# A hybrid recurrence and feed-forward block: second norm turned by DMA inside SBUF, first transfers issued ahead of the parity branch

## The chip, the cores and the metric

The kernel runs on the 8 cores of one Trainium2 chip. Its time is the device time, in microseconds, of the slowest core; the figure for a kernel is the median of its runs. Cores 0 to 3 are one die, cores 4 to 7 the other. Even and odd cores run two different programs of one kernel, chosen by a branch on the parity of the core's number.

## What is computed

The input x is 4 sequences of 4096 tokens, 1024 wide, in float32. Cut to what matters:

```python
h = rmsnorm(x, norm_mix_g)
q, f, i, g, c, bg, xb, ga, gb = split(h @ w_in)       # 4x512, 3x512, 2x1024
y_a = hgrn2_mixer(q, f, i, g) @ w_branch_a           # gated linear recurrence, 4 heads of 128x128
y_b = (bg * causal_conv3(c * xb)) @ w_branch_b       # depthwise, 3 taps
x = x + (sigmoid(ga) * y_a + sigmoid(gb) * y_b) @ w_out
h2 = rmsnorm(x, norm_ffn_g)                          # "the second norm"
x = x + (silu(h2 @ w_gate) * (h2 @ w_up)) @ w_down   # inner width 2816
out = rmsnorm(x, norm_final_g)
```

## The kernel before, in words

Each pair of cores takes one sequence. The even core computes its first 2152 tokens, the odd core the last 1944. The recurrence carries a state over the whole sequence, so the odd core first runs a short pre-scan over the tokens before its own (projections f and i only), which gives it the state to begin with; the even core has no such part. `BL_EVEN` and `BL_ODD` (lines 18 and 19) cut the tokens into blocks of tiles, as (tiles, rows of a tile): even (4,128), (4,128), (3,128), (3,128), (3,120); odd (4,128) three times and (4,102). The pre-scan of the odd core uses the even cut.

All matmuls are bf16 with float32 sums in PSUM, which has 8 banks of 512 columns. Most projections have the weights as the stationary operand and 128 channels of up to 512 tokens as the moving one (`mm_fm`, line 823, its matmuls recorded at L830); some are token-major (`mm_tok`, L841). Weights lie in HBM as float32 slabs of 128x4096 (2 MB), and are cast to bf16 on the way into a ring of 8 slots by DMAs that the pool engine issues (`load_next`, line 697, recorded at L714 and in tables as ring<-wall). Their order is `LOADS` (line 418). A slab is loaded into a slot once its former user has released it; the first slabs are cut in quarters, and a quarter can be gated on the arrival of an x tile.

The stages: (1) the first norm. An x tile (128 tokens by 1024 channels, 512 KB) is loaded by SP (`load_more`, line 742, L747, ring<-xall); ACT squares and sums it, ACT makes the reciprocal root, DVE scales it into bf16, and `transp` (line 852) turns it: TensorE transposes eight 128x128 pieces into a PSUM bank (L859) and DVE multiplies them by the norm weight on the way to `hT` (L810). (2) conv projections (`conv_gen`, line 1047), beside the norm of the next block; on odd cores also the pre-scan (`pf_gen`, `pt_gen`, `pv_gen`). (3) per block the dense projections of the recurrence and its core, merged with the first half of the gates (`gates_gen`, line 1313). (4) the second half of the gates of block b+1, merged with `d_gen` of block b (line 1358): the output projection, the residual sum x1, its store to HBM (`x1spill`, L1378), the load of the next x tile (L1354), and the second norm. For each pair of tiles this is a square and a reciprocal root on ACT, a scaling on DVE into one of two buffers in `rtmp`, and `transp` into `hT`. The buffer of a tile is also what the square of the tile after next writes. (5) the feed-forward projections (`ffn_gen`, line 1410); the last block of stage 4 is merged with their start. (6) the down projection with the final norm (`down_gen`, line 1437).

The order on each engine is fixed at build time. The generators are merged by their costs (`merge`, line 371) into a list of operations with their reads and writes; `schedule` (line 180) then plays the list through a model: each operation has a duration, a DMA takes its `nbytes` at `DMA_RATE` = 310e3 bytes a microsecond and `DMA_LAT` = 2.2 us more, and the next operation of an engine is the one that can start first. `pick` gives each PSUM result the bank that was freed longest ago (two neighbouring banks where a result needs a pair). `run` (line 309) issues the order, with a wait on a semaphore for each dependency not yet known to be met. Each of the five engine queues takes the branch in `emit_both` (line 339) first, and everything of the program stands behind it.

At the start six small ACT operations (L774 to L778) and two on DVE make the constants of the forget gate. They stand ahead of the first norm in the list.

## Time and profile before

| | us |
|---|---|
| median of 3 runs (lowest, highest) | 1015.64 (1014.77, 1016.02) |
| the profiled execution | 1016.44 |
| its span, core 4 (first to last instruction of the slowest core) | 1014.9 |
| spans of even cores 0, 2, 6 | 1011.2, 1010.7, 1011.0 |
| spans of odd cores 1, 3, 5, 7 | 1011.2, 1012.0, 1009.9, 1009.5 |
| busy on core 4: TensorE, DVE, ACT | 974.9, 435.5, 376.3 |

Times below are in us from the span's start on the core named. PE is TensorE; SPq, POOLq and the like are an engine's own queue; "issue" is time in which the profile shows nothing that the engine waits for. "[3.16 <-DMA ring<-wall]" behind a row is the time that the engine sat idle before it, and what ended that.

### The profile page before, as it was taken

The page shows a single profiled execution, that of the slowest core. Times are in us where ns is not written, and L with a number is a line of the kernel's source. Part 1 is how long each engine was busy: PE and PEld are TensorE (multiplying, and loading weights), DVE is VectorE, ACT ScalarE, POOL GpSimd, SP SyncE. Part 2 cuts the span into 40 slices and gives each one's busy share as a digit, 9 for nine tenths or more (in the row PEclk, how much of TensorE's full clock was granted, in tenths as well). Part 3 has the DMA queues.
Part 4 walks back from the last instruction along what each step waited for, and adds up shares of the span by engine and source line. Part 5 has one row for each costly group of instructions (what it writes and reads, how often), then busy time and mean ns, then how long its engine had stood idle before and what let it go on. Part 6 is the DMA issues. An engine that isn't in the chain of part 4 may idle for free.

```text
span 1014.9 us, 15424 instructions; the slowest of 8 cores (1009.5 to 1014.9 us)
## 1 busy us (share of the span) xinstructions
PE 974.9 (96%) x5574; PEld 526.6 (52%) x5574; DVE 435.5 (43%) x678; ACT 376.3 (37%) x668; POOL 24.6 (2%) x52
## 2 busy tenths in 40 slices
PE   0889999999999999999999999999999999999997
PEld 0435646455556554455555645555464655444455
DVE  3535467776877664566544212122221212223223
ACT  3434285948586742445534111111111111111112
POOL 2000000000000000000000000000000000000000
PEclk9999999999999999999999999999999999999999
DMA  6982405100003544334387040203003053323112
GB/s 125 237 199 46 79 1 94 33 1 2 1 1 55 113 97 112 116 119 140 124 176 150 1 84 1 43 1 64 21 5 79 2 125 125 125 106 119 63 63 59
DMA packets 18947, 78.74 MB, mean 78 GB/s; under 512 B 2224, under 2 KB 2224, under 8 KB 15792
## 3 DMA queue, kind: packets, MB, share of 16 engines
q0 software_dynamic: 6336, 33.03, 18.5%
q1 hardware_dynamic: 12393, 44.38, 13.2%
q8 instruction: 49, 0.80, 0.3%
q14 instruction: 34, 0.28, 0.1%
q10 hardware_dynamic: 135, 0.25, 0.1%
HBM read 93.05 MB, written 17.63 MB: 109 GB/s over the span
## 4 chain that ended last, share of the span: by engine, by line
PE 90%; DMA 4%; ACT 2%; issue 2%; DVE 1%; SPq 1%; POOL 0%; ACTq 0%; DVEq 0%; POOLq 0%
PE pf L830 60%; PE pf L1454 16%; PE pf L841 10%; DMA ring<-wall 3%; DMA ring<-xall 1%; ACT arena L806 1%; PE pf L859 1%; PE pf L1079 1%; SPq L747 0%; ACT L806 0%; PE pf L1254 0%; PE pf L1256 0%; PE pf L1215 0%; PE pf L1234 0%; PE pf L1304 0%
## 5 line engine op out<-in xcount | busy, mean ns | idle before, releaser
L830 PE MATMUL pf<-hT,ring 128*128 128x384 bf16 (+2 forms) x3200 | 607.8, 346 | 6.4 <-DMA ring<-wall 3.2
L830 PEld LDWEIGHTS pf<-hT,ring 128*128 128x128 bf16 x3200 | 311.9, 98 | 273.2 <-issue 11.3
L1454 PE MATMUL pf<-ring,arena 128*128 128x512 bf16 (+2 forms) x735 | 159.8, 373 | 0.0
L806 ACT ACTIVATE rtmp<-pf 128x512 f32<-128x512 f32 (+2 forms) x114 | 59.9, 531 | 203.2 <-PE pf L830 196.5
L1454 PEld LDWEIGHTS pf<-ring,arena 128*128 128x128 bf16 (+1 forms) x735 | 76.2, 105 | 78.1
L810 DVE TENSOR_TENSOR arena<-rtmp,pf 128x512 bf16<-128x512 f32 (+2 forms) x85 | 51.7, 609 | 143.1 <-PE pf L830 129.5
L806 ACT ACTIVATE arena<-pf 128x512 f32<-128x512 f32 (+11 forms) x145 | 77.7, 572 | 75.5 <-PE pf L830 68.8
L830 PE MATMUL pf<-arena,ring 128*128 128x512 bf16 (+2 forms) x320 | 70.8, 345 | 1.5 <-ACT arena L806 1.4
L806 ACT ACTIVATE rtmp<-hT 128x1024 bf16<-128x1024 f32 (+3 forms) x19 | 18.4, 967 | 130.7 <-DVE hT L810 130.7
L841 PE MATMUL pf<-ring,hT 128*128 128x512 bf16 (+1 forms) x272 | 62.6, 379 | 0.0
L806 ACT ACT_TABLE_LOAD x44 | 56.5, 1283 | 6.6 <-DVE sso L1262 3.7
L841 PE MATMUL pf<-ring,arena 128*128 128x512 bf16 (+1 forms) x248 | 58.4, 379 | 0.0
L810 DVE TENSOR_TENSOR hT<-pf,hT 128x512 f32<-128x512 f32 (+2 forms) x35 | 23.7, 676 | 80.3 <-PE pf L1454 80.3
L818 DVE SCALAR_TENSOR_TENSOR arena<-arena,pf 128x512 f32<-128x512 f32 (+2 forms) x54 | 32.2, 600 | 34.9 <-PE pf L830 23.4
L806 ACT ACTIVATE rtmp<-arena 128x1024 bf16<-128x1024 f32 (+4 forms) x27 | 27.0, 1000 | 51.9 <-DVE arena L818 51.9
L810 DVE TENSOR_TENSOR hT<-pf,cst_sb 128x1024 bf16<-128x1024 bf16 (+1 forms) x34 | 40.4, 1206 | 9.0 <-PE pf L859 8.9
L830 PEld LDWEIGHTS pf<-arena,ring 128*128 128x128 bf16 x320 | 30.4, 98 | 26.0 <-issue 1.8
L810 DVE TENSOR_TENSOR arena<-U,pf 128x512 bf16<-128x512 f32 (+2 forms) x27 | 16.3, 604 | 62.0 <-PE pf L830 60.1
L841 PEld LDWEIGHTS pf<-ring,hT 128*128 128x128 bf16 (+1 forms) x272 | 28.1, 104 | 28.1
L714 POOL DMA_DIRECT2D ring<-wall x44 | 23.4, 532 | 791.3 <-PE pf L830 590.8
L810 DVE TENSOR_TENSOR arena<-arena 128x512 bf16<-128x512 f32 (+8 forms) x46 | 36.9, 801 | 9.2 <-ACT arena L806 6.6
L810 DVE TENSOR_TENSOR arena<-Wt,pf 128x512 bf16<-128x512 f32 (+2 forms) x25 | 15.1, 603 | 56.9 <-PE pf L830 56.9
(101 smaller groups left out, 572.9 us busy)
## 6 DMA issues: line engine op xcount, KB each, us to landing
ring<-wall POOLq DMA_DIRECT2D x24, 1024.0 KB, 11.4
ring<-xall SPq DMA_DIRECT2D x14, 512.0 KB, 8.7
arena<-xall SPq DMA_DIRECT2D x14, 512.0 KB, 4.4
x1spill<-arena SPq DMA_DIRECT2D x14, 512.0 KB, 3.0
hT<-x1spill SPq DMA_DIRECT2D x14, 512.0 KB, 4.4
out<-hT SPq DMA_DIRECT2D x14, 512.0 KB, 2.6
ring<-wall POOLq DMA_DIRECT2D x12, 256.0 KB, 10.6
ring<-wall POOLq DMA_DIRECT2D x6, 512.0 KB, 5.8
```

The source lines that it names most:

```text
L714: P.dma("pool", lambda E, s=s, idx=idx, a=a, z=z: E.dma_start(out=ring[s][:, a:z], in_=w_d[idx][:, a:z]), reads=need(gates[q]) if q < len( ...
L806: P.op("act", lambda E: E.activation(out=rs(out), in_=rs(in_), func=func, **kw), reads=reads, writes=writes, dur=dur, aset=ASET[func] if f ...
L810: P.op("dve", lambda E: E.tensor_tensor(out=rs(out), in0=rs(a), in1=rs(b), op=op), reads=reads, writes=writes, dur=0.17 + width(out, a, b) ...
L818: P.op("dve", lambda E: E.scalar_tensor_tensor(out=rs(out), in0=rs(a), scalar=s, in1=rs(b), op0=op0, op1=op1), reads=reads, writes=writes, ...
L830: last = E.matmul(pb(bk)[:, 0:ncol], lhsT=sl[:, o_:o_ + 128], rhs=rhs[:, c, :], start=(c == 0), stop=(c == kc - 1))
L841: last = E.matmul(pb(bk)[0:w, :], lhsT=lhs(c), rhs=rhs_list[c], start=(c == 0), stop=(c == n - 1))
L859: last = E.transpose(out=tbv.res()[:, c * w:(c + 1) * w], in_=xs[:, c * 128:(c + 1) * 128], identity=ident[0:w, 0:w])
L1079: last = E.matmul(pb(by)[:, 0:T], lhsT=diagw[:, k * 4 + m, :], rhs=u[:, m, k:k + T], start=(k == 0), stop=(k == 2))
L1454: last = E.matmul(pb(bk)[0:CH, 0:w], lhsT=act_v(c)[:, r0:r0 + CH], rhs=rl[c], start=(c == 0), stop=(c == 21))
```

## The change

In `d_gen`, tiles whose row count is a multiple of 16 are turned by a new function `dma_transp`: one transposing DMA, issued by SP, from the bf16 tile in `rtmp` straight into `hT` in SBUF, and a DVE multiply by the norm weight in place in `hT`. Those are the full tiles of 128 rows. The last block's tiles, now 124 rows on even cores and 100 on odd ones, still go through TensorE. The first x loads, the constants' load and the first two slabs' loads (the operations of SP and POOL listed before `P.mark()`) are issued by each queue before it takes the branch; for this the slabs lie in HBM in the order of each parity's `LOADS`. The gate constants are made after the first norm. The list of the odd program merges conv and pre-scan in another way. `schedule` keeps one aligned pair of banks free on even cores and packs single results next to held banks on odd ones. The areas of the feed-forward result `act` are laid out anew, per block. The even core computes 2164 tokens, the odd one 1936. Cut to its core:

```diff
 
 D = 1024
 DFF = 2816
-BL_EVEN = [(4, 128), (4, 128), (3, 128), (3, 128), (3, 120)]
-BL_ODD = [(4, 128), (4, 128), (4, 128), (4, 102)]
+BL_EVEN = [(4, 128), (4, 128), (3, 128), (3, 128), (3, 124)]
+BL_ODD = [(4, 128), (4, 128), (4, 128), (4, 100)]
 NP = len(BL_EVEN)
 TOK_EVEN = sum(n * w for n, w in BL_EVEN)
 TOK_ODD = sum(n * w for n, w in BL_ODD)
 NCST = 39
 
 KB = 1024
-ARENA = 88 * KB + 288
+ARENA = 88 * KB
 HT_BYTES = 16 * max(TOK_EVEN, TOK_ODD)
 
 
...
             self._newsem(chan.dsem)
         self._add(eng, fn, reads, writes, 0.6 if eng == "pool" else 0.1, None, chan.dsem, nbytes)
 
-    def schedule(self, nbanks, window=48, hold=6.0):
+    def mark(self):
+        self.pre = [o.i for o in self.ops if o.eng in ("sp", "pool")]
+        for i in self.pre:
+            self.ops[i].prio = i - 1e6
+
...
             for k in range(0, nbanks - n + 1, n):
                 if any(held[k:k + n]):
                     continue
-                t = max(bank_free[k:k + n])
-                if best is None or t < best[0]:
-                    best = (t, k)
-            return best
+                if strict and not oldest:
+                    rest = [h or k <= j < k + n for j, h in enumerate(held)]
+                    if not any(not rest[j] and not rest[j + 1] for j in range(0, nbanks, 2)):
+                        continue
+                key = (not strict and n == 1 and not held[k ^ 1] and not oldest, max(bank_free[k:k + n]))
+                if best is None or key < best[0]:
+                    best = (key, k)
+            return None if best is None else (best[0][1], best[1])
 
         while left:
             while head_pe < len(pend_pe) and pend_pe[head_pe] in done_pe:
                 if not avail[e]:
                     continue
                 cand = sorted(avail[e], key=lambda i: ops[i].prio)[:window]
+                if e == "pe" and head_pe < len(pend_pe) and pend_pe[head_pe] in avail[e] and pend_pe[head_pe] not in cand:
+                    cand.append(pend_pe[head_pe])
+                if pre_left[e]:
+                    first = min(i for i in self.pre if ops[i].eng == e and ops[i].fin is None)
+                    cand = [i for i in cand if i == first]
                 rows = []
                 for i in cand:
                     o = ops[i]
...
 def emit_both(block, odd, even):
     odd.number()
     even.number()
+    assert odd.pre == even.pre
+    for i in odd.pre:
+        assert odd.val[i] == even.val[i] and odd.ops[i].deps == even.ops[i].deps
 
     def run(E, e):
+        known = {}
+        odd.run(E, e, known, 0)
         pid = E.partition_id()
         with E.If(pid & 1):
-            odd.run(E, e)
+            odd.run(E, e, dict(known), 1)
         with E.Else():
-            even.run(E, e)
+            even.run(E, e, dict(known), 1)
 
     @block.tensor
     def _(E):
...
-        fits = 22 * 2 * TOK <= ARENA
-
-        def act_at(j):
-            return ("arena", 2 * TOK * j) if fits or j < 21 else ("misc", 0)
-
-        act_b = [[reg(f"act{j}_{b}", act_at(j)[0], act_at(j)[1] + 2 * OFF[b], 2 * TB[b]) for b in range(NB)] for j in range(22)]
-
-        def act_v(j):
-            sp, o_ = act_at(j)
-            return (arena if sp == "arena" else misc)[:, o_ // 2:o_ // 2 + TOK]
+        act_off = {}
+        at = {"arena": 0, "misc": 0}
+        for j in range(22):
+            for b in range(NB):
+                sp = "arena" if at["arena"] + 2 * TB[b] <= ARENA else "misc"
+                act_off[j, b] = (sp, at[sp])
+                at[sp] += 2 * TB[b]
+        assert at["misc"] <= 6144
+        act_b = [[reg(f"act{j}_{b}", *act_off[j, b], 2 * TB[b]) for b in range(NB)] for j in range(22)]
+
+        def act_v(j, b):
...
             name = LOAD_ORDER[nxt["i"]]
             nxt["i"] += 1
             slot_of[name] = s
-            idx = names.index(name)
+            idx = nxt["i"] - 1
             parts = SLABS[name]
             if len(parts) == 2:
                 cuts = [(0, 2048, b_ring[s][0:2]), (2048, 4096, b_ring[s][2:4])]
                                                base=0, channel_multiplier=1), reads=[b_idf], writes=[b_idf])
         load_next([None, None, xm[0], xm[1]], 4)
         load_next([xm[1], xm[2], xm[3], xm[3]], 4)
+        P.mark()
         xgate.update({4: xm[3], 5: b_ring[slot_of[LOAD_ORDER[0]]][3]})
         xgate.update({6 + q: b_ring[slot_of[LOAD_ORDER[1]]][q] for q in range(4)})
         for _ in range(2):
...
+        def gate_consts():
+            P.op("dve", lambda E: E.tensor_tensor(out=sv[:, :, 3], in0=cst[:, L0:L0 + 4], in1=cst[:, L1:L1 + 4], op=ALU.subtract),
+                 reads=[b_cst], writes=[b_sv])
+            for k, sg in ((1, -1.0), (0, 1.0)):
...
             tt(dst[:, :, t * w:(t + 1) * w], tbv[:, 0:8 * w].rearrange("p (c t) -> p c t", t=w),
                cst[:, gcol:gcol + 8].rearrange("p (c o) -> p c o", o=1).to_broadcast([128, 8, w]), ALU.mult,
                [tb.buf, b_cst], b_dst)
+
+        ch_tr = bufs("dtr", 4)
+
+        def dma_transp(xs, b_xs, gcol, dst, b_dst, t, w):
+            out = dst[:, :, t * w:(t + 1) * w]
+            P.dma("sp", lambda E: E.dma_start_transpose(out=out, in_=xs), reads=[b_xs], writes=b_dst, chan=cyc("dtr", ch_tr),
+                  nbytes=524288)
+            tt(out, out, cst[:, gcol:gcol + 8].rearrange("p (c o) -> p c o", o=1).to_broadcast([128, 8, w]), ALU.mult,
+               b_dst + [b_cst], b_dst)
 
         xj = {"n": 0}
 
                         xm_, b_xm = x1D[m % 4]
                         xs_, b_xs = xsD[m % 2]
                         ts(xs_[0:CH, :], xm_[0:CH, :], stat[0:CH, k + i, 1:2], 0.0, b_xm + [b_stat[k + i]], [b_xs])
-                        transp(xs_[0:CH, :], b_xs, G2, hTs[b], [b_hT[b][tm]], tm, CH)
+                        (dma_transp if CH % 16 == 0 else transp)(xs_[0:CH, :], b_xs, G2, hTs[b], [b_hT[b][tm]], tm, CH)
                     yield 1.5
 
         SLS = [(single(12), b_T[12]), (single(13), b_T[13]), (U[:].rearrange("p h d -> p (h d)"), b_U), (Wt[:].rearrange("p h d -> p (h d)"), b_W)]
...
         npre = lambda i: norm_gen(hp(i)[0], lambda t: [b_hpre[i % 2][t]])
         if odd:
             drain(npre(0))
+            gate_consts()
             P.op("dve", lambda E: E.tensor_copy(out=hcol[:, :, 0:1], in_=hp(0)[0][:, :, 1:2]), reads=[b_hpre[0][0]], writes=[b_hcol])
             P.op("dve", lambda E: E.tensor_copy(out=hcol[:, :, 1:2], in_=hp(0)[0][:, :, 0:1]), reads=[b_hpre[0][0]], writes=[b_hcol])
             merge((seq(pf_gen(0), pv_gen(0)), 13.8), (npre(1), 2.5))
             merge((seq(pf_gen(1), pt_gen(0), pv_gen(1)), 16.2), (npre(2), 2.5))
             load_next([xm[14]])
             merge((seq(pf_gen(2), pt_gen(1), pv_gen(2)), 16.2), (norm_gen(hTs[0], mn(0)), 2.5))
-            merge((seq(halo_gen(), conv_gen(0, P1S)), 26.0), (npre(3), 2.5))
-            merge((seq(pf_gen(3), pt_gen(2), pv_gen(3)), 16.2), (norm_gen(hTs[1], mn(1)), 2.5))
-            merge((conv_gen(1, P1S), 23.4), (npre(4), 2.5))
-            merge((seq(pf_gen(4), pt_gen(3), pv_gen(4)), 16.2), (norm_gen(hTs[2], mn(2)), 2.5))
-            merge((conv_gen(2, P1S), 23.4), (norm_gen(hTs[3], mn(3)), 2.5), (pt_gen(4), 2.5))
+            merge((seq(halo_gen(), conv_gen(0, P1S)), 26.0), (seq(npre(3), norm_gen(hTs[1], mn(1))), 5.0))
+            merge((conv_gen(1, P1S), 23.4), (seq(pf_gen(3), pt_gen(2), pv_gen(3)), 12.5), (seq(npre(4), norm_gen(hTs[2], mn(2))), 5.0))
+            merge((conv_gen(2, P1S), 23.4), (seq(pf_gen(4), pt_gen(3), pv_gen(4)), 12.5), (norm_gen(hTs[3], mn(3)), 2.5))
+            drain(pt_gen(4))
         else:
             drain(norm_gen(hTs[0], mn(0)))
+            gate_consts()
             load_next([xm[5], xm[6], xm[7], xm[7]], 4)
             late_consts()
             for b in range(NB - 1):
         release("wo0", "wo1")
         drain(E_)
         down_gen()
-        P.schedule(8)
+        P.schedule(8, not odd)
         P.finals = b_out
     return P
```

## Rows read from the trace of the kernel before

**Rows 1.** The page: busy tenths of TensorE in 40 slices of the span, core 4.

```profile
PE   0889999999999999999999999999999999999997
```

**Rows 2.** Spans and granted TensorE clock of the cores.

```profile
core 0: 1011.2 us, clock 0.997
...
core 3: 1012.0 us, clock 0.991
core 4: 1014.9 us, clock 0.997
```

**Rows 3.** Chain that ended last, core 4: start, duration, what.

```profile
2.82 4.36 issue
7.17 4.59 SPq L747
```

**Rows 4.** Timeline of core 4's start: start, duration, engine, line, operation.

```profile
17.39 1.06 ACT L806 ACTIVATE arena<-ring 128x1024 bf16<-128x1024 f32 x1 [7.98 <-DMA ring<-xall]
...
20.23 0.28 ACT L806 ACTIVATE stat<-stat,cst_sb 128x1 f32<-128x1 f32 x1
...
29.88 8.69 PE L830 MATMUL pf<-hT,ring 128*128 128x512 bf16 x32 [1.48 <-DVE hT L810]
...
57.82 4.49 PE L830 MATMUL pf<-hT,ring 128*128 128x512 bf16 x14 [3.16 <-DMA ring<-wall]
```

**Rows 5.** Timeline of core 5's start.

```profile
2.56 0.41 SPq L747 DMA_DIRECT2D ring<-xall  x1
...
7.03 1.06 ACT L806 ACTIVATE arena<-ring 128x1024 bf16<-128x1024 f32 x1 [2.62 <-DMA ring<-xall]
...
19.03 1.22 DVE L810 TENSOR_TENSOR arena<-pf,cst_sb 128x1024 bf16<-128x1024 bf16 x1
```

**Rows 6.** Timeline of core 4, TensorE in the second norm.

```profile
434.55 1.06 PE L859 MATMUL pf<-ident,rtmp 128*128 128x128 bf16 x16
435.44 1.89 PE L841 MATMUL pf<-ring,arena 128*128 128x512 bf16 x8
```

**Rows 7.** Stretches: PE, PEld, DVE, ACT, POOL busy; clock, DMA share, GB/s; core 4, then 5.

```profile
5.00:14.00 9.00, 0.00 (x0) 0.00 (x0) 2.77 (x10) 1.49 (x2) 1.95 (x5) 1.00 0.45 45
14.00:30.00 16.00, 4.17 (x33) 3.23 (x34) 10.68 (x22) 7.58 (x22) 3.19 (x6) 1.00 1.03 228
...
5.00:14.00 9.00, 1.83 (x16) 1.54 (x16) 5.78 (x19) 5.79 (x17) 2.39 (x5) 1.00 1.06 286
14.00:30.00 16.00, 9.84 (x148) 9.13 (x147) 8.46 (x12) 7.91 (x16) 1.06 (x2) 0.90 1.02 224
```

**Rows 8.** Waits of TensorE on core 3: total, times, longest.

```profile
PE pf L841 <- DMA ring<-wall: 3.5, 1, 3.5
PE pf L841 <- DVE hT L810: 2.0, 2, 1.4
```

**Rows 9.** Groups of instructions of core 4 by shape: busy, mean ns, idle before.

```profile
L810 DVE TENSOR_TENSOR hT<-pf,cst_sb 128x1024 bf16<-128x1024 bf16 x28 | 33.6, 1218 | 5.6 <-PE pf L859 5.5
...
L810 DVE TENSOR_TENSOR arena<-arena 128x1024 f32<-128x1024 f32 x4 | 4.9, 1222 | 0.2
```

**Rows 10.** SP's queue on core 4: first and 14th store of x1.

```profile
401.22 0.33 SPq L1378 DMA_DIRECT2D x1spill<-arena  x1
...
511.63 0.33 SPq L1378 DMA_DIRECT2D x1spill<-arena  x1
```

**Rows 11.** DMA issues of core 4: count, KB of each, median us to landing.

```profile
x1spill<-arena SPq DMA_DIRECT2D x14, 512.0 KB, 3.0
...
ring<-wall POOLq DMA_DIRECT2D x12, 256.0 KB, 10.6
```

**Rows 12.** The stretch of core 4 with 14 full tiles of the second norm.

```profile
400.00:512.00 112.00, 112.00 (x668) 60.81 (x667) 66.22 (x96) 50.71 (x84) 0.00 (x0) 1.00 0.38 123
```

**Rows 13.** Chain of core 4: eight matmuls of 512 columns, eight of 384.

```profile
84.57 1.73 PE pf L830 x8
...
104.05 1.30 PE pf L830 x8
```

More of the change, by code:

```diff
@@ L122, in __init__ @@
         self.lead = 0
+        self.pre = []
         for e in ENGS:
@@ L201, in schedule @@
         left = len(ops)
+        pre_left = {e: sum(1 for i in self.pre if ops[i].eng == e) for e in ENGS}
+        pre_set = set(self.pre)
         for o in ops:
@@ L255, in schedule @@
             avail[e].remove(i)
+            if i in pre_set:
+                pre_left[e] -= 1
             for v in o.vbs:
@@ L307, in number, with run @@
                     self.val[i] = ("P_" + e, n)
-    def run(self, E, e):
+    def run(self, E, e, known, part):
         ops, val = self.ops, self.val
-        known = {}
         own = "P_" + e
-        for i in self.order[e]:
+        npre = sum(1 for i in self.pre if ops[i].eng == e)
+        for i in self.order[e][:npre] if part == 0 else self.order[e][npre:]:
             o = ops[i]
@@ L330, in run @@
                 o.fn(E).then_inc(self.sems[own], 1)
-        if e == "sp":
+        if e == "sp" and part == 1:
             for b in self.finals:
@@ L598, in build_prog @@
             b_hpre.append(reg_group([f"hpre{i}t{t}" for t in range(4)], "arena", O_OG + i * 8192, 8192))
-        UO = O_OG + 16384 if odd else O_MG
+        UO = 16 * max(TOK_EVEN, TOK_ODD)
         u_v, b_u = area("u", UO, 4112)
@@ L1449, in down_gen, with fn @@
                     rl = [fd[hf][c // 8][0][:, (c % 8) * 512 + o0:(c % 8) * 512 + o0 + w] for c in range(22)]
-                    def fn(E, bk=bk, rl=rl, r0=r0, w=w, CH=CH):
+                    def fn(E, bk=bk, rl=rl, r0=r0, w=w, CH=CH, nb=nb):
                         last = None
                         for c in range(22):
-                            last = E.matmul(pb(bk)[0:CH, 0:w], lhsT=act_v(c)[:, r0:r0 + CH], rhs=rl[c],
+                            last = E.matmul(pb(bk)[0:CH, 0:w], lhsT=act_v(c, nb)[:, r0 - OFF[nb]:r0 - OFF[nb] + CH], rhs=rl[c],
                                             start=(c == 0), stop=(c == 21))
@@ L1591 @@
     SLABS = slab_table()
-    wall = np.zeros((len(SLABS), 128, 4096), f32)
-    for i, parts in enumerate(SLABS.values()):
-        for kind, key, r0, kc, c0, nc_, off in parts:
-            w = W[key][r0:r0 + kc * 128, c0:c0 + nc_].reshape(kc, 128, nc_)
-            if kind == "rhs":
-                w = w.transpose(1, 0, 2)
-            else:
-                w = w.reshape(kc, 128, nc_ // 128, 128).transpose(1, 2, 0, 3)
-            wall[i, :, off:off + kc * nc_] = w.reshape(128, kc * nc_)
+    walls = {}
+    for odd in (True, False):
+        wall = np.zeros((len(SLABS), 128, 4096), f32)
+        for i, name in enumerate(LOADS[odd]):
+            for kind, key, r0, kc, c0, nc_, off in SLABS[name]:
+                w = W[key][r0:r0 + kc * 128, c0:c0 + nc_].reshape(kc, 128, nc_)
+                if kind == "rhs":
+                    w = w.transpose(1, 0, 2)
+                else:
+                    w = w.reshape(kc, 128, nc_ // 128, 128).transpose(1, 2, 0, 3)
+                wall[i, :, off:off + kc * nc_] = w.reshape(128, kc * nc_)
+        walls[odd] = wall
     in_maps = []
@@ L1609 @@
             xall[0:TOK_EVEN] = x[b, 0:TOK_EVEN]
-        in_maps.append({"xall": xall, "cst": cst, "gf": gf, "wall": wall})
+        in_maps.append({"xall": xall, "cst": cst, "gf": gf, "wall": walls[half == 1]})
     nc = _get_nc()
```

22 lines of the change are left out of this document (11 added, 11 removed).

## Prediction

> **What bounds the kernel now.** I read the page's first two parts, the cores, the chain of the slowest core, then its first 60 us and the stretch with the second norm. TensorE's slices are full, nine tenths or more, except at the two ends [rows 1]: outside the start, time goes only where TensorE's work goes. Even cores and odd cores run two programs and end together: core 4 (even) sets the end at 1014.9 us, core 0 (even) ends at 1011.2, the last odd one, core 3, at 1012.0 [rows 2]. A gain on one parity alone is capped by the other: at about 3 us. The profiled execution took 1016.44 us, 1.5 more than its span, and 0.8 more than the median of 1015.64; I sum against 1016.44 and take off 0.8 at the end.
>
> At the start of core 4 the chain stands in "issue" until 7.17, spends 4.59 in the first x load's issue and then goes through loads of x and of slabs [rows 3]. The first square begins at 17.39; the first projection matmul at 29.88; six constant operations lie between the square's end, 18.45, and its reciprocal root at 20.23; TensorE waits once more, 3.16 us, at 57.82 [rows 4]. Core 5, with the same first tiles, issues its first load at 2.56 in 0.41 us and begins its square at 7.03; the multiply of its fourth tile starts at 19.03 [rows 5]. So the even program's data are 10 us late, and the difference is in how late the queues reach the first issue.
>
> In the second norm each pair of tiles costs TensorE 16 matmuls, from 434.55 to 435.44 [rows 6]. Nothing waits for them: they are paid because TensorE is full.
>
> **The change, part by part.**
>
> *First transfers ahead of the branch.* Five SP issues and eight POOL issues move before the branch. On even cores tile 0 then arrives as on core 5: its square at 7.03 instead of 17.39, 10.4 earlier. Fourth tile: 19.03 + 1.2 of its multiply gives 20.3 for the first projection against 29.88, a gain of 9.6. What could take some back: ACT, DVE and TensorE still pass the late branch; ACT then stands ready when SP does now, at 7.17 [rows 3] or a little later, 1 or 2 us behind core 5's first square, with slack before the fourth tile. SP and POOL pass it after their early issues. SP's next load is gated on tile 3, which lands before its square and so some 4 us ahead of 19.03, about 15; if the branch and its late first issue cost it what they cost now (4.36 + 4.59 [rows 3]) from about 4.5, it is ready at 13.5. POOL is free at about 17 and its next slab waits for x tiles far behind that. From then on DMA bounds: its share is 1.03 on core 4 from 14 us and 1.06 on core 5 from 5 us [rows 7], so core 4's stream begins about 9 earlier. Do two busy cores slow each other? Core 5 moved 286 GB/s while core 4 moved 45, and 224 when both were busy, but then with casting weight loads, which count their half-size output [rows 7]; so between no slowing and a fifth. A fifth of the 30 us behind 29.88 would be 6 us; the sum of both cores' shares is full either way, so I take 1.5. Term on even cores: −8, bounds −3 and −11 (the last with the 3.16 wait gone too, on core 4). On odd cores: 0 at best, +3 at worst, for TensorE there waits 3.5 for a slab [rows 8]; I take +1.
>
> *Constants after the first norm.* Six ACT operations, 18.45 to 20.23, 1.8 us [rows 4], leave the stretch between the first square and its rsqrt. The fourth tile comes later than that backlog lasts, so I count 0, at most −1.8; if the cover goes, +1.8 where they are next due, at the gates.
>
> *Turning by DMA.* Off TensorE: 0.89 us per pair, 0.445 a tile [rows 6]. Even: blocks 4+4+3+3, 14 full tiles, −6.2. Odd: 12 tiles, −5.3. The short tiles (124 and 100 rows) stay on TensorE. The DVE multiply stays, now out of SBUF: from PSUM it takes 1218 ns, and the nearest row within SBUF with a float32 operand 1222 [rows 9]: 0 us. SP issues one more DMA a tile, between the x1 store and the next x load, at about 0.4 us each; it issues two in 8.5 us now, 401.22 to 511.63 for 14 tiles [rows 10]: hidden. But a wait appears: SP stands until the scaled tile is ready, and queued behind it are the next x1 store and x load. In the planner's order a store comes 4 us or more after; hidden while that order holds. The larger wait is DVE's: it stands on the landing, and behind it are the evictions of gates and of the output projection, for which TensorE's banks wait. The planner gives the transfer 524288/310000 + 2.2 = 3.9 us, so DVE stands in vain only beyond that. No row shows such a transfer. From below: a 512 KB store lands in 3.0 us; from above: 256 KB of weights under load, 10.6 [rows 11]. I take the store's, the nearest in kind (SP's queue, plain bytes, twice the size), and so 0. DVE has room: 66.22 of 112 us busy [rows 12], so of the 17 us of a pair it works 10 and has 7 free. The square of the tile after next writes the buffer that the transfer reads; it comes after 8 us, also covered.
>
> A transfer can be worse than the bytes say. The Trainium skill, "VectorE: DVE Perf Modes", section "The three transpose paths", gives the DMA path 1309 ns for one 128×128 block and TensorE 390; "Advanced Engine Details and Errata", section "X-Bar Transpose (TRN2)", says such DMAs are as fast as regular ones. By the first, eight blocks in turn would be 10.5 us, an estimate from that page's figure, and the sum would be rival 4's; by the second it would stay as it is. For TensorE the trace disagrees with the 390: 56 ns here [rows 6]; on the DMA path no row decides.
>
> *Blocks 120→124 (even) and 102→100 (odd).* A column costs (1.73−1.30)/(8×128) us = 0.42 ns [rows 13]. Matmuls whose width is the block's: feed-forward 352, conv 108, dense 64, gates 192, together 716. Even: 716×12×0.42 ns = +3.6. Odd: 716×8×0.42 = −2.4; its pre-scan grows by 0.2.
>
> *Planner and merges.* Even: a pair of banks is kept free. The slices show no wait that it could mend in full [rows 1], and a lost tenth in a slice of 25 us would be 2.5: I take −0.5, bounds −3 and +3. Odd: conv and pre-scan run side by side. Of TensorE's waits it can fill the 2.0 on the turned norm [rows 8] and smaller ones like it, which I put at as much again; against it stands packing singles next to held partners, which reuses a bank soon after its eviction. I take −2, bounds −5 and +4. Activation placement, slab order in HBM and the arena size move no time: same bytes, same instructions.
>
> **Sum.** Even, core 4: 1016.44 −8 −6.2 +3.6 −0.5 = 1005.3. Odd, core 3: 1012.0+1.5 = 1013.5, −5.3 −2.2 +1 −2 = 1005.0. Less 0.8: 1004.5 and 1004.2. The later one: **1004.5**. The other even cores come out about 4 lower.
>
> **Rivals.** (1) *The start stays bound by loads.* With both cores of a pair drawing from 3 us on, the slabs come late and even cores keep only 4 of the 8. For it: the share is already full and core 4 alone waits for a slab. Against: core 4 got 228 GB/s and core 5 224 in the same stretch. Time: 1008.5. (2) *The odd program becomes the bound*, its slab 3 later and its bank reuse costing 4 instead of giving 2: 1004.2 + 2 + 6 = 1012. Against: its waits are short, and every term but these two is a gain. (3) *Every bound good*: core 4 −11 −6.2 +3.6 −3 gives 999.0; odd −5.3 −2.2 −5 gives 1000.2, and so about 1000. (4) *Slower*: the turns take 10.6 us each, one after the other, 21.2 for a pair. DVE stands 17.3 beyond plan where it has 7 free, so the stage lengthens 10.3 on each of 6 pairs, 62 us: 1066. The turning point: the gain of 11 is used up when the stage grows 1.9 a pair, at a landing of 3.9+7+1.9 = 12.8 us for a pair, 6.4 a tile. For it: the 10.6 row, whose KB are the same as a turned tile's. Against: the DMA share there is only 0.38 [rows 12]. A part of (4) may also come as a small loss, 5 to 8 us, inside my range. That the turns stay on TensorE cannot be: 128 is a multiple of 16.
>
> **The numbers.** Main case 0.60 (1001 to 1008), rival 1 0.14, rival 2 0.08, rival 3 0.07, rival 4 0.11. The range 999 to 1012 leaves out rival 4 and the edges. A measurement tells about 0.2% from no change, 2 us: faster than 1013.6 has 0.86, between 1013.6 and 1017.7 0.04 (rival 2 with a small stall), above 0.10.
>
> **What would show it.** Right: core 4's first SP load at about 2.5 and its first projection matmul at 20 to 22; in the second norm only the 24 matmuls of the three short tiles left; transfers landing in 3 to 5 us; TensorE busy 100% from 400 to 512; spans within 4 us between parities. Wrong: POOL or SP issuing their first load behind the branch late (4 us or more after tile 3 lands); "ring<-wall" waits of 5 us and more on even cores; DVE's waits on the turned tile over 7 us a pair with TensorE waiting on evictions behind them; an odd core last by more than 3 us.

## The result, and the profile after

The changed kernel took 1035.73 us (1034.56 to 1036.36) where the one before took 1015.2 beside it: a ratio of 1.0203 [1.0185, 1.0221]. The forecast was 1004.5 with a range of 999 to 1012. The profiled execution took 1036.32; its slowest core is now core 2. Executions in which a die ran slower at a lower granted clock are left out everywhere.

First the spans of the changed kernel's cores, as in [rows 2].

```profile
core 2: 1034.4 us, clock 0.987
core 3: 1004.6 us, clock 0.988
core 4: 1032.7 us, clock 0.987
core 5: 1002.9 us, clock 0.990
```

The odd cores did what was forecast: core 3's sum of 1005.0 is a span of 1003.5. The even ones, all four, lost about 21 us, and their granted clock fell from 0.997 to 0.987. So there is a stall, and the clock falls with it. The page's slices of core 2 show where, beside [rows 1]:

```profile
PE   1999999999999999999993999999999999999995
...
PEclk9999999999999999999996999999999999999998
```

Slice 22 begins at 21/40 of 1034.4, at 543 us: the end of the second norm, where slices before were full. Stretches of core 2 there (busy time and count of PE, PEld, DVE, ACT and POOL; clock; DMA share; GB/s):

```profile
540.00:545.00 5.00, 3.37 (x16) 1.34 (x14) 0.00 (x0) 0.00 (x0) 0.00 (x0) 1.00 1.00 170
545.00:550.00 5.00, 0.00 (x0) 0.00 (x0) 0.00 (x0) 0.00 (x0) 0.00 (x0) 0.63 0.59 120
550.00:555.00 5.00, 0.00 (x0) 0.00 (x0) 0.00 (x0) 0.00 (x0) 0.00 (x0) 0.50 0.26 90
555.00:560.00 5.00, 0.00 (x0) 0.00 (x0) 4.08 (x5) 2.97 (x6) 0.00 (x0) 0.50 0.26 106
560.00:565.00 5.00, 3.99 (x16) 1.99 (x17) 2.54 (x3) 1.84 (x2) 0.00 (x0) 0.50 0.21 85
```

The chain of core 2 through the same place (start, duration, what):

```profile
514.42 0.70 DVE arena L848
...
519.18 36.12 DMA arena<-xall
...
562.00 8.15 PE pf L860 x30
```

and its timeline (idle time before, and what ended it, in brackets):

```profile
526.01 31.00 SPq L1417 DMA_DIRECT2D x1spill<-arena  x2
...
555.39 1.29 DVE L848 SCALAR_TENSOR_TENSOR arena<-pf,arena 124x512 f32<-124x512 f32 x2 [18.05 <-DMA arena<-xall]
...
561.01 0.98 PE L889 MATMUL pf<-ident,rtmp 124*128 124x124 bf16 x8 [17.64 <-DVE rtmp L844]
```

One load of x, a tile of 124 rows and 496 KB, takes 36 us. The residual add waits for it, then the norm, then the turn on TensorE, and TensorE stands 17.6 us. The stretches say how the load runs: from 550 us on the share of the 16 DMA engines is 0.26, though this load and the stores of such tiles behind it are all that there is to do. Queue of SP on core 2 from 550 to 555 us (packets, MB, share), the only one that moves anything:

```profile
q1 hardware_dynamic: 114, 0.45, 25.6%
```

That is four engines out of 16, always busy. Few engines alone do not make 36 us: at 0.45 MB in 5 us the 496 KB would be through in some 5.5 us, an estimate from this row. Until some 549 us slab loads use the same engines. From 540 to 545 us they have 93.8% of them with 106 packets, and SP's queue moves 27 packets, 0.11 MB. Over four of 16 engines 106 packets are 26.5, so the two queues go about packet for packet there. A load on few engines next to slabs is what takes 36 us. In the kernel before, TensorE on core 0 was busy 5.00 of the 5 us from 555 to 560.

The rest of the loss is smaller. Up to 392.7 us core 2 is level with before. Its feed-forward begins at 562.00 instead of 547.09 (+14.9) and lasts 4.5 longer, and behind its last matmul there are 10.6 us instead of 6.3. Of these, the last store's landing takes 7.4 us with 124 rows (issued by 1027.01, end of the span 1034.4) and took 3.0 with 120 (1007.71, 1010.7). Together +23.7.

The turning transfers are about as cheap as was assumed, in the groups of DMA issues of two stretches of core 2 (count, median us to landing):

```profile
hT<-rtmp SPq DMA_TRANSPOSE x2, 3.2
...
hT<-rtmp SPq DMA_TRANSPOSE x1, 24.4
```

The first row is of 409 to 416 us, where 2114 packets carry two turns; of the 14 turns, the median landing is 3.3 us, against the 3.0 of [rows 11] from which it was taken. The second is the 14th turn, at 508.2, beside three slab loads of 1 MB that POOL issued from 503.7 to 506.8. The queues of that stretch, 508 to 532 us (packets, MB, share of 16 engines):

```profile
q0 software_dynamic: 410, 2.97, 85.2%
q1 hardware_dynamic: 1123, 0.61, 34.1%
```

The slabs' packets are 7 KB each on average, the turns' some 250 B (the 0.52 MB of two turns over 2114 packets). On odd cores the last pair of turns meets the same slabs. Timeline of core 3:

```profile
535.55 21.02 SPq L900 DMA_TRANSPOSE hT<-rtmp  x2
...
560.75 3.43 PE L871 MATMUL pf<-ring,arena 128*100 128x512 bf16 x8 [6.12 <-DVE arena L840]
```

At the start, the first load is issued early as meant, and it brings little. Timeline of core 4, answering to [rows 4]:

```profile
1.07 0.42 SPq L774 DMA_DIRECT2D ring<-xall  x1
...
13.62 0.06 DVE L756 MEMSET zw<- 128x1 f32 x1 [13.62 <-issue]
...
27.31 0.16 DVE L809 TENSOR_SCALAR sv<-sv 128x4 f32<-128x4 f32 x1
...
27.54 4.00 PE L860 MATMUL pf<-hT,ring 128*128 128x512 bf16 x9 [1.48 <-DVE sv L809]
```

The first projection matmul is at 27.54 instead of 29.88, not at 20 to 22; the wait of 1.48 us before it is as long as it was. DVE comes out of the branch at 13.62 us; on the four even cores it does so at 11.2 to 14.8, where it did at 6.3 to 7.8 before. On core 5 it does so at 3.26.

### The profile page after: what moved, and what is told of

The parts are those of the page before. It is cut to its first block, busy times and chain, and to the rows that moved or that the text cites. A ratio compares the mean times of both kernels' runs of the same rounds, so it can differ in the third digit from the quotient of the medians.

```text
span 1034.4 us, 15226 instructions; the slowest of 8 cores (1002.9 to 1034.4 us)
## 1 busy us (share of the span) xinstructions
PE 975.4 (94%) x5462; PEld 520.6 (50%) x5462; DVE 435.9 (42%) x678; ACT 374.7 (36%) x666; POOL 24.7 (2%) x52
## 4 chain that ended last, share of the span: by engine, by line
PE 88%; DMA 3%; ACT 3%; issue 2%; DVE 2%; SPq 0%; DVEq 0%; ACTq 0%
PE pf L860 59%; PE pf L1493 16%; PE pf L871 10%; DMA arena<-xall 3%; ACT arena L836 1%; PE pf L1118 1%; PE pf L889 1%; ACT L836 0%; PE pf L1254 0%; SPq L1417 0%; PE pf L1295 0%; PE pf L1293 0%; PE pf L1273 0%; ACT rtmp L836 0%; DVE arena L840 0%
## 5 line engine op out<-in xcount | busy, mean ns | idle before, releaser
L1493 PE MATMUL pf<-ring,arena 128*128 128x512 bf16 (+2 forms) x722 | 157.3, 374 | 0.0
L840 DVE TENSOR_TENSOR hT<-pf,hT 128x512 f32<-128x512 f32 (+2 forms) x35 | 23.7, 676 | 80.3 <-PE pf L1493 80.3
L848 DVE SCALAR_TENSOR_TENSOR arena<-pf,arena 128x512 f32<-128x512 f32 (+1 forms) x34 | 23.4, 690 | 49.1 <-PE pf L871 25.6
L741 POOL DMA_DIRECT2D ring<-wall x44 | 23.5, 534 | 804.4 <-PE pf L860 609.5
L836 ACT ACTIVATE Wt<-pf 128x512 f32<-128x512 f32 (+2 forms) x27 | 14.4, 532 | 67.4 <-PE pf L860 67.4
## 6 DMA issues: line engine op xcount, KB each, us to landing
ring<-wall POOLq DMA_DIRECT2D x12, 256.0 KB, 11.4
```

What stands on the lines that cost most here:

```text
L741: P.dma("pool", lambda E, s=s, idx=idx, a=a, z=z: E.dma_start(out=ring[s][:, a:z], in_=w_d[idx][:, a:z]), reads=need(gates[q]) if q < len( ...
L836: P.op("act", lambda E: E.activation(out=rs(out), in_=rs(in_), func=func, **kw), reads=reads, writes=writes, dur=dur, aset=ASET[func] if f ...
L840: P.op("dve", lambda E: E.tensor_tensor(out=rs(out), in0=rs(a), in1=rs(b), op=op), reads=reads, writes=writes, dur=0.17 + width(out, a, b) ...
L848: P.op("dve", lambda E: E.scalar_tensor_tensor(out=rs(out), in0=rs(a), scalar=s, in1=rs(b), op0=op0, op1=op1), reads=reads, writes=writes, ...
L1493: last = E.matmul(pb(bk)[0:CH, 0:w], lhsT=act_v(c, nb)[:, r0 - OFF[nb]:r0 - OFF[nb] + CH], rhs=rl[c], start=(c == 0), stop=(c == 21))
```

## Experiments

Ratios are against the kernel before on the same chip, with a 95% interval. Spans are medians over the four cores of a parity and over all runs; the kernel before has 1010.3 to 1010.5 on even cores and 1008.8 to 1009.6 on odd ones on these chips.

| kernel | even | odd | time | ratio |
|---|---|---|---|---|
| after | 1032.3 | 1003.3 | 1035.73 | 1.0203 [1.0185, 1.0221] |
| e1, last full block turned on TensorE | 1025.5 | 999.6 | 1031.71 | 1.0202 [1.0179, 1.0225] |
| e2, all turned on TensorE | 1033.0 | 1003.2 | 1036.47 | single run |
| e3, slabs wait for the turns | 1027.4 | 995.4 | 1030.42 | 1.0185 [1.0167, 1.0204] |
| e4, slabs in 2 KB packets | 1027.6 | 996.6 | 1030.79 | single run |
| e5, last tiles of 120 and 102 rows | 1000.7 | 1006.5 | 1009.61 | 0.9969 [0.9958, 0.998] |
| e6, 124-row transfers cut 112 + 12 | 1005.0 | 1001.3 | 1009.16 | 0.9964 [0.9952, 0.9976] |
| e8, e5 with no early issue | 1003.2 | 1005.8 | 1008.27 | 0.9955 [0.9939, 0.9971] |
| e9, e5 with SP alone early | 1000.9 | 1006.0 | 1008.26 | 0.9955 [0.9938, 0.9971] |
| e10, e5 and slabs wait | 1000.8 | 1005.0 | 1009.94 | 0.9969 [0.9957, 0.998] |
| e11, before and the turns alone | 1004.9 | 1001.1 | 1007.87 | 0.9949 [0.9935, 0.9964] |
| e12, e5 with all turned on TensorE | 1005.9 | 1010.8 | 1014.30 | 1.0011 [1.0002, 1.0021] |
| e13, e5 with the old bank rule on even cores | 1003.3 | 1006.5 | 1009.44 | 0.9959 [0.9944, 0.9974] |
| e14, e10 with 102-row transfers cut 96 + 6 | 1000.5 | 997.6 | 1003.40 | 0.9907 [0.989, 0.9923] |
| e15, before with 102-row transfers cut 96 + 6 | 1010.5 | 1003.2 | 1012.78 | 1.0 [0.9989, 1.001] |

**First question: do the turning transfers hold up the load of x?** The 14th turn lands late beside the slabs, and the next load of x is behind it in SP's queue. Theory A blames the turn, and four kernels take it away in different ways.

e1 turns the last full block on TensorE:

```diff
-(dma_transp if CH % 16 == 0 else transp)(xs_[0:CH, :], ...
+(dma_transp if CH % 16 == 0 and b < NB - 2 else transp)(xs_[0:CH, :], ...
```

> The changed kernel with the full tiles of the last full block (3 of 14 on even cores, 4 of 12 on odd) turned on TensorE again. Theory A (the last turning DMA is in flight beside three 1 MB slab loads, creeps, and holds the x load behind it in SP's queue: 18 + 2 us idle on even cores, 6 on odd): both stalls go, even cores end at 1034 - 20 + 1.3 = about 1013 to 1016 at most, odd cores at about 1000 to 1003. Rival B (the planner's bank rule or the new order starves TensorE there, whoever turns): even cores stay above 1025.

e2 turns all on TensorE:

```diff
-(dma_transp if CH % 16 == 0 else transp)(xs_[0:CH, :], ...
+transp(xs_[0:CH, :], ...
```

> The changed kernel with every tile turned on TensorE; start, block sizes, bank rules and merges as changed. Theory A: the stall is gone; even cores pay 6.2 us for the turns back: 1034 - 20 + 6 = about 1018 to 1020, odd cores 1005 - 6 + 5 = 1004. Rival B: even cores 1035 or more, with TensorE idle near 545 us as before.

e3 lets the three slabs released at that point wait until the last full tile is turned:

```diff
-        release("ga1", "wab1", "gb1")
+        release("ga1", "wab1", "gb1", gate=b_hT[NB - 2][BL[NB - 2][0] - 1])
```

> The changed kernel, but the three slabs that are loaded when the second half of the gates is done wait until the last full tile has been turned and multiplied. All 14 turns stay on DMA. Theory A: the last turn lands in 3 to 4 us instead of 24, the x load behind it in under 10, TensorE has no idle time over 3 us there; even cores about 1012 to 1014. Rival C (the turn is slow whenever two follow close on the x1 store and load, slabs or not): landing stays over 15 us and the even cores above 1025.

e4 leaves their time as it is and cuts each in four transfers of 2 KB packets:

```diff
-        release("ga1", "wab1", "gb1")
+        release("ga1", "wab1", "gb1", ncut=4)
```

> The changed kernel, but those three slabs are each loaded by four DMAs of 256 KB, whose packets are 2 KB long instead of 8 KB (0.17 us instead of 0.62 us of an engine); same bytes at the same time. Theory A1 (a DMA engine serves the two queues a packet each in turn, so each of the turn's 64 short packets per engine waits for one long one): the last turn's landing falls from 24 us to about 64 x 0.17 + 3 = 10 to 14 us and the idle time of TensorE from 18 to under 8. Rival A2 (the queues share by bytes, or the slabs simply take the engines in full until they are done): landing stays above 20 us.

The chains of core 2 in e3 and in e4, and of core 0 in e2, where nothing at all is turned by DMA:

```profile
512.44 38.74 DMA arena<-xall
```

```profile
514.02 35.19 DMA arena<-xall
```

```profile
519.06 36.12 DMA arena<-xall
```

Theory A fell for the even cores: they stay at 1025 and more, and the load takes 30 to 39 us on every even core of the four kernels. It was not all wrong there: e1, e3 and e4 end 5 to 7 us earlier than the changed kernel. The held turn delays the issue of the load, which on core 2 comes at 519.18 in the changed kernel and at 512.44 in e3. e2 has no held turn either, and its turns on TensorE cost about what that wins (their price is under the fourth question). e4's turn lands in 19.5 us on core 2, where 10 to 14 or over 20 were expected. On odd cores gating the slabs is worth 8 us. How long core 3's 12 turns take to land, first in the changed kernel, then in e3:

```profile
DMA to landing us min/median/max: 3.1/3.2/23.4
```

```profile
DMA to landing us min/median/max: 3.1/3.3/5.3
```

and no wait of TensorE is left there between 400 and 700 us. The collision is real, and on core 3 it is the whole of the wait. Cutting the slabs in smaller packets gives as much (996.6), though the longest landing on core 3 is still 17.5 us; why that one costs TensorE nothing was not taken apart.

**Second question: is it the number of rows?** In the changed kernel the share is four engines of 16. A last tile has 124 rows on even cores now and had 120. 124 divides by 4 and by nothing between 4 and 16; 120 divides by 15. Theory D: a transfer of SP's queue goes over as many engines as divide its rows. The Trainium skill says so, in "DMA: Bandwidth & Descriptors", section "Why a DMA increments its semaphore by 16 and not by 1": the largest number up to 16 that divides the slowest dimension of both sides; it gives 10 for 100 rows. Two kernels test it, the second without touching the bytes.

e5:

```diff
-BL_EVEN = [(4, 128), (4, 128), (3, 128), (3, 128), (3, 124)]
-BL_ODD = [(4, 128), (4, 128), (4, 128), (4, 100)]
+BL_EVEN = [(4, 128), (4, 128), (3, 128), (3, 128), (3, 120)]
+BL_ODD = [(4, 128), (4, 128), (4, 128), (4, 102)]
```

> The changed kernel with the last blocks as before, 3x120 rows on even cores and 4x102 on odd ones; turns by DMA, early issue, bank rules and merges as changed. Theory D (a DMA of SP's queue is spread over as many engines as divide its rows, at most 16: 124 rows over 4, 120 over 15, so each load of a 124-row tile takes some 36 us and TensorE waits for it): the stall near 540 us goes; even cores 1034 - 19 (stall) - 2 (slow clock behind it) - 2.4 (columns up to there) - 1.8 (feed-forward columns) - 4 (last store on 15 engines) = about 1003 to 1007; odd cores about 1005 to 1008 (102 rows over 6 engines, 2.4 us more columns). Rival E (the bank rule or the order delays the x load): even cores stay above 1025.

e6 keeps 124 and 100 rows and issues every plain transfer of 124 rows as one of 112 and one of 12 (16 and 12 engines by the theory):

```diff
+            mk(E, 0, 112).then_inc(self.sems[chan.dsem], 16)
+            return mk(E, 112, 124)
...
-cnt[o.chan] = cnt.get(o.chan, 0) + 16
+cnt[o.chan] = cnt.get(o.chan, 0) + (32 if o.two else 16)
```

> The changed kernel with its 124-row tiles kept, but each DMA of such a tile (x loads, x1 store and load, output) issued as two, rows 0 to 111 and rows 112 to 123. Same bytes, same computation. Theory D: 112 rows go over 16 engines and 12 over 12, so the x load lands in under 12 us (the three slabs beside it), the stall goes, even cores about 1007 to 1011. Rival E: above 1025, because what is computed and its order are as in the changed kernel.

Both even spans came out 2 us below what was expected, 1000.7 and 1005.0. The odd cores take the even cut in their pre-scan, so e6 cuts three loads there as well.

TensorE on core 0 in stretches (busy and count, clock, DMA share, GB/s), the changed kernel and then e6:

```profile
545.00:550.00 5.00, 0.00 (x0) 0.57 0.27 90
550.00:555.00 5.00, 0.00 (x0) 0.50 0.25 104
555.00:560.00 5.00, 2.23 (x12) 0.50 0.26 105
```

```profile
545.00:550.00 5.00, 5.00 (x33) 1.00 0.38 75
550.00:555.00 5.00, 5.00 (x33) 1.00 0.00 0
```

Same rows, same bytes, 27.3 us less on the even cores (1032.3 to 1005.0). Theory D is shown. That it takes the slabs beside the load as well is read from the stretches of 540 to 555 us. No run has a load of 124 rows without them: those that e3 gates are issued at 511 us, just ahead of its load. The clock tells the same: in the stop it falls to 0.50, its level of 1.2 GHz, and on core 2 it is still there from 560 to 565 us, when TensorE is busy 3.99 of 5 again; in the stretches of e6 it is at 2.4 GHz.

e6 against e5 also prices the block sizes themselves: 4 columns more per short tile, and two issues for each of its transfers, cost the even cores 4.3 us.

**Third question: what is the early issue worth?** e8 issues nothing ahead of the branch, e9 only SP's part; both with the 120 and 102 rows of e5.

```diff
-        self.pre = [o.i for o in self.ops if o.eng in ("sp", "pool")]
+        self.pre = []
```

> As e5, and no transfer is issued ahead of the branch (each queue takes the branch first, as before). Theory F (code of the compute engines is fetched by DMA and, with the data loads started first, waits behind them, so the early issue gains nothing on even cores): DVE's first instruction on even cores at about 5 to 8 us instead of 14.8, first x tile squared at about 15, first projection matmul at 27 to 29, time within 2 us of e5. Rival G (the early issue gains its 8 us somewhere else): e8 is 5 us or more slower than e5.

```diff
-        self.pre = [o.i for o in self.ops if o.eng in ("sp", "pool")]
+        self.pre = [o.i for o in self.ops if o.eng == "sp"]
```

> As e5, but only SP's loads (four x tiles, constants) are issued ahead of the branch; the pool queue's two slabs behind it. Theory F: less data is in the engines ahead of the code, so DVE starts at 8 to 11 us on even cores, the first projection matmul comes at 22 to 26, and even cores end 2 to 5 us before e5's. Rival: DVE still starts at 14 to 15 (x tiles alone delay the code as much) and nothing is gained.

Start of core 2 in e8:

```profile
5.86 3.84 SPq L774 DMA_DIRECT2D ring<-xall  x1
6.16 0.06 DVE L756 MEMSET zw<- 128x1 f32 x1 [6.16 <-issue]
```

and the waits of e5 and of e9 there, for DVE's first instruction:

```profile
DVE zw L756 <- issue: 13.5, 1, 13.5
```

```profile
DVE zw L756 <- issue: 11.1, 1, 11.1
```

With no early transfers DVE starts at 6.2, with all of them at 13.5. What is in the queues while DVE waits: core 2 of the kernel before, from 3 to 9 us, and of the changed one, from 9 to 17 us (packets, MB, share of 16 engines):

```profile
q14 instruction: 7, 0.06, 4.8%
```

```profile
q0 software_dynamic: 383, 0.70, 66.5%
q1 hardware_dynamic: 243, 0.86, 35.8%
q14 instruction: 4, 0.03, 1.2%
```

Instructions come by DMA, over the same engines as the data. In the changed kernel none of their packets is seen from 3 to 9 us, where the data queues have 96% of the engines. What was to be gained by data that come earlier is paid by code that comes later. e8 came out as expected. In e9 DVE starts at 10.3 to 11.4 and the first square is at 11.9 to 13.0, but the first projection only at 27.0 to 28.8, where 22 to 26 was expected, and the even cores win nothing on e5, where 2 to 5 us were. In e9 core 4 even stops in mid-stream, at TensorE's turns of the first norm:

```profile
21.37 1.33 PE L889 MATMUL pf<-ident,arena 128*128 128x128 bf16 x11 [3.10 <-issue]
```

The even cores keep 2.5 us of the early issue (1003.2 to 1000.7), the odd ones lose 0.7, within their scatter. The time of e8, e9 and e5 is the same within their intervals, since the odd cores set it. That fetches wait behind data is read from these traces and from the order of the three kernels; no run changed the fetches alone. The Trainium skill, "Runtime: NRT & Kernel Launch", section "Instruction fetch mechanics", has each sequencer fetch its code by a DMA queue of its own. It calls the cost of running on from block to block mostly hidden, and warns that a taken branch to code not yet fetched waits for a fetch. The trace agrees with the warning: behind this branch DVE starts at 6.2 to 13.5 us, with packets of the instruction queue in between.

**Fourth question: what are the parts worth once the stall is gone?** e11 is the kernel before with `dma_transp` and its call, and nothing else of the change; e12 is e5 with the edit of e2; e13 is e5 without this on the even cores:

```diff
-                if strict and not oldest:
-                    rest = [h or k <= j < k + n for j, h in enumerate(held)]
-                    if not any(not rest[j] and not rest[j + 1] for j in range(0, nbanks, 2)):
-                        continue
```

> The kernel before with the turning DMAs and nothing else of the change. The prediction's step for the turns: 14 tiles on even cores take 6.2 us of TensorE away, 12 on odd cores 5.3. So even spans near 1005 us where they were 1011. With the collision beside the slabs the odd cores keep less: if the 4 to 6 us wait before the FFN stands here too, odd spans stay at 1010 to 1012 and the time is within 2 us of before. Rival (turns are worth nothing even where nothing collides, since TensorE only waits elsewhere): even spans stay at 1010 to 1012 too.

> All of the change but the turns, with last tiles of 120 and 102 rows: every tile is turned on TensorE. If the turns are worth 6.2 us on even cores, their spans rise from 1000 to 1001.5 to about 1006 to 1007; the odd cores lose 5.3 us and win back the 4.6 us wait, and stay at 1004 to 1006. The time is then 1 to 2 us above the kernel with turning DMAs, a ratio of 0.997 to 0.999. Rival (the gain of the even cores comes from the bank rule, turns are worth little): even spans stay at 1000 to 1002.

> Last tiles of 120 and 102 rows, and on the even cores the planner gives PSUM banks out by the rule of the kernel before; the odd cores are as they were. The prediction's step for the planner: 0.5 us on even cores, so their spans rise by less than 1 us from 1000 to 1001.5, and the ratio stays at 0.996 to 0.998. Rival (the bank rule carries the even cores' gain): their spans rise by 4 us or more, to 1005 or above.

e11's even cores came out as expected; its odd ones had been put at 1010 to 1012 and have 1001.1. e12's odd cores had been put at 1004 to 1006 and have 1010.8, so there the turns are worth more than was thought. In e13 2.6 us lies between the theory (under 1) and the rival (4 or more).

On even cores the turns are worth 5.5 (e11 against before) and 5.2 (e12 against e5), early issue 2.5 (e8), the bank rule 2.6 (e13): 10.3 to 10.6, and e5 stands 9.8 below before. On odd cores the turns are worth 8 in the kernel before and 4.3 in e5. The 8 is more than the 5.3 of matmuls: part of it is that the wait of 4.4 us for `DVE rtmp L814` before the feed-forward became one of 2.5 for a residual add, on core 3. Without the turns the change costs the odd cores 1.8 (e12 against before); which of its parts does, merges or bank order or early issue, was not tried. e10 puts the gate of e3 on e5.

> Last tiles of 120 and 102 rows, and the three slabs that are loaded while the second norm ends wait until the last full tile is turned. Theory (a turn's small packets creep behind the slabs' large ones, and the rows decide how many engines carry a tile): the longest landing of a turn falls from 20 to 24 us to under 6 us on every core, the 4.6 us wait of TensorE on the odd cores before the FFN goes, so odd spans fall from 1004 to 1007 us to 998 to 1001 us; even spans stay at 1000 to 1001 us; the time is about 1004 us on a chip whose kernel before takes 1012.9, a ratio of 0.990 to 0.992. Rival (the wait on the odd cores comes from elsewhere, or slabs that start 20 us later are missed by the FFN): odd spans stay at 1004 to 1007 us, the ratio at 0.996 to 0.997, or a new wait on the ring stands in TensorE's waits near the FFN's start.

It missed: the odd cores gained 1.5, not 6, and scattered from 997 to 1011. Turns landed in 5.2 at most; but the chain of core 3 and its timeline have this:

```profile
553.84 26.00 DMA arena<-xall
```

```profile
581.96 7.40 PE L860 MATMUL pf<-hT,ring 128*128 128x512 bf16 x24 [6.20 <-DVE arena L848]
```

A load of x again, 408 KB of 102 rows. 102 divides by 6 and by nothing between 6 and 16. The kernel before had this wait all along, on its odd cores. So there was one open question left: is the gain of the odd cores from 102 to 100 rows (10 engines) the same cause as the loss of the even ones? e14 cuts the 102-row transfers of e10 in 96 and 6 rows, e15 does it in the kernel before; the edit is that of e6 with these numbers, and in e14 the gate of e3 too.

> The kernel with last tiles of 120 and 102 rows and the slabs gated (even cores 1000.8 us, odd 1005.0), with each plain transfer of a 102-row tile on the odd cores issued as 96 and 6 rows. Theory (102 rows go over 6 DMA engines as 124 go over 4, and that transfer, 26.0 us long, is what the gated odd cores wait for): the transfer lands within 15 us, the wait of TensorE before the FFN's last tile (6.2 us on core 3) goes, and the odd spans fall to 996 to 999 us; even spans stay at 1000 to 1002. The time is then near 1004 to 1005 us where the kernel before takes 1013, a ratio of 0.991 to 0.993. Rival (the odd cores lose their time to the turns and the slabs still, or to the early issue): odd spans stay at 1004 to 1007 and the ratio at 0.996 to 0.997.

> The kernel before, with nothing but its 102-row transfers cut in 96 and 6 rows. Its odd cores wait 4.0 to 4.4 us for a square of the last block that waits for such a transfer. Theory (engines by the row count): that wait goes and odd spans fall from 1009 to 1004 to 1006 us; even spans stay at 1010.4, so the time stays within 0.2% of before. Rival (that wait comes from the three slabs of 8 KB packets beside it): odd spans stay at 1008 to 1011.

Waits of TensorE on core 3 between 300 and 900 us: before, then e15, then e14.

```profile
PE pf L859 <- DVE rtmp L814: 4.6, 2, 4.4
```

```profile
PE pf L871 <- DVE rtmp L826: 0.8, 2, 0.6
```

```profile
PE pf L872 <- ACT arena L848: 1.1, 1, 1.1
```

Both as the theory had it: the odd cores fall by 6.4 in the kernel before, and by 7.4 on e10. e15's time stays, since its even cores set it. e14 is faster than both kernels: 1003.40, 0.9907 of before. In its profiled execution all cores are within 5 us; die 0:

```profile
core 0: 1000.9 us, clock 0.999
core 1: 999.2 us, clock 0.991
core 2: 1000.3 us, clock 0.999
core 3: 997.0 us, clock 0.993
```

## Why the prediction was wrong

**Blocks 120→124 and 102→100: the step that failed.** It charged the new sizes by matmul columns alone, "716×12×0.42 ns = +3.6". That term was right: 4.3 measured. What it left out is that each plain transfer of a short tile has its row count too: loads of x, spills and reloads of x1, output stores. 124 rows put them on 4 engines where 120 had 15, beside slab loads: +27.3 on the even cores. The prediction's term for that was nothing, without a reason. The kernel before held the clue. On core 3 TensorE waits 4.4 us at the second norm's end for a tile whose load has 102 rows and takes 23.5 us (e15 takes that wait away); the prediction took two rows of that list [rows 8] and left out this one, the longest behind the start. Where a size is changed, every instruction that carries it has to be priced, DMAs as well as matmuls.

**Rivals.** Rival 4 came out on the right side by the wrong cause: it had TensorE wait for turns of 10.6 us, and a turn lands in 3.3. None of the rivals had the x load. The 0.10 for slower was all that stood for such a thing.

**First transfers ahead of the branch: mis-sized.** −8 was taken for the even cores, 2.5 was measured. The step compared with core 5, which has no late branch, and put ACT, DVE and TensorE "1 or 2 us behind". DVE came out of the branch 4.0 to 8.5 us later than before on the four even cores, it seems because what it waits for is itself a transfer. Rival 1 (−4) was nearer in size and blamed the slabs. For odd cores +1 was taken, and 0.7 measured.

**Constants after the first norm: 0, with 1.8 if the cover goes.** The traces fit the 0. The row before the first projection names the constants' last step, `DVE sv L809` at 27.31, but the wait is 1.48 us as it was in [rows 4], and the multiply of the turned tile ends at 27.39, later than that step began. From the first square to the first projection it is 12.4 us on core 4 where it was 12.5. No run moved them back.

**Turning by DMA: right.** −6.2 on even cores, 5.2 to 5.5 measured; −5.3 on odd ones, 4.3 in e5, where the collision costs a wait of 4.4 us. The landing was taken as 3.0 and is 3.3. SP's issue was taken at 0.4 us a tile and is 1.25: hidden as well, while nothing crowds the queues. Of the two sections of the Trainium skill weighed there, this case is nearer to "X-Bar Transpose (TRN2)", by which a transposing transfer is as fast as a regular one: 3.3 us for 256 KB, where a plain store of 512 KB takes 3.0. It is far from the prediction's estimate of 10.5 from the other. The danger was named ("DVE's waits on the turned tile") but at the wrong place: not from turn to turn, but where slabs of the weights are released. The 256 KB row of 10.6 us in [rows 11] was the sign that transfers beside slabs take long, and the sum set it aside.

**Planner: −0.5 on even cores, 2.6 measured** within bounds of −3 and +3. On odd cores its share wasn't taken apart.

**The sum.** Put together as measured, the even cores come to 1010.5 −5.5 −2.5 −2.6 +4.3 = 1004.2, and e6, the change with the transfers mended, has 1005.0; the forecast for core 4 was 1003.8 as a span. That these agree is mostly luck. The terms promised 11.1 and brought 6.3: early issue 5.5 too good, turns and columns 0.7 each, planner 2.1 too bad. What cancelled this is that the sum started from core 4 of the profiled execution, 4.4 above a typical even core. The other even cores, forecast 4 lower, missed by 5. Even so e6's time is 1009.2, not 1004.5: the slowest of eight cores, at 1007.2, is above the typical one. The range to 1012 would have held that. It did not hold the term that was not there.

## What to carry to other kernels

Price a change of tile height on every transfer that carries it, by the largest divisor of its rows up to 16: 112 + 12 or 96 + 6 rows in two transfers beat 124 or 102 in one. A DMA share that rests on a round fraction of 16 engines while somebody waits is the sign. Read the share of the stretch beside the wait, not the mean, and mind that large loads beside it hide it: here the share was 1.00 until 545 us. Transfers of small packets that somebody waits for want to be kept apart in time from large slabs, and transfers moved to the very start compete with the code of the engines that are to use them.

## What had not been expected of the hardware

Beside weight slabs a load of 124 rows in 4 KB rows took 36.12 us and one of 102 rows 26.00. Once the slabs were done the share of the DMA engines was 0.26 in the stretch with the 124-row load and the stores behind it; several such transfers did not raise it, so they seem to share the same four engines. A transposing transfer of a 128x1024 bf16 tile within SBUF landed in 3.3 us, cost SP's queue 1.25 us of issue and came as some 1050 packets of about 250 B. Beside weight slabs the same transfer landed in up to 24.7 us (e11, core 3), and SP's queue was held for 14.6 us by its issue. And an engine's first instruction behind a branch came at 6.2 us or at 13.5, on the same core, with no data transfer started ahead of the branch or with those of SP and POOL.
